# Weaving neighbouring weight blocks word by word in a two-layer kernel on one core

## What is computed

```python
# first block: modulated layers
u = h @ w_in                       # layer 0: gated linear recurrence
mix = (recurrence(conv(u)) * gelu(u)) @ w_out
x = x + g_m * mix
x = x + g_f * ((silu(h @ w_gate) * (h @ w_up)) @ w_down)
q, k, v = h @ w_q, hk @ w_k, hk @ w_v   # layer 1: attention, then w_o and a second swiglu
# second block: 16 extra tokens in front (272 in all), two hybrid layers
proj = h @ w_in                    # convolution, state space, retention, stick-breaking
up = [branch_n @ w_branch[n] for n in range(4)]
mix = sum(sigmoid(gate_n) * up_n) @ w_out
f = (silu(h @ w_ffn_gate) * (h @ w_ffn_up)) @ w_ffn_out
```

## Time and profile before

| | |
|---|---|
| median of three executions | 2205.68 us (2205.02 to 2208.81) |
| span of the profiled execution, first to last instruction | 2205.2 us |
| TensorE busy with matmuls | 2182.8 us, 99% of the span |
| TensorE busy with weight loads | 2129.4 us, 97% |
| DVE / ACT busy | 1542.7 us (70%) / 1169.5 us (53%) |
| moved by DMA | 428.19 MB, mean 194 GB/s |

### The profile page before, as it was taken

The page is one execution under the profiler, slowest core; times in us unless marked ns, Lnnn a source line. Parts: engine busy times, 40 slices in busy tenths (PEclk is TensorE's granted clock), DMA queues, the critical chain, the costliest instruction groups (busy, mean ns, idle before and its releaser), DMA issues.

```text
span 2205.2 us, 40768 instructions
## 1 busy us (share of the span) xinstructions
PE 2182.8 (99%) x17030; PEld 2129.4 (97%) x17030; DVE 1542.7 (70%) x2584; ACT 1169.5 (53%) x1950; POOL 2.2 (0%) x6
## 2 busy tenths in 40 slices
PE   8999999999999999999999999999999999999999
PEld 6899999999999999999999999999999999999998
DVE  6878997776577678755655865596879556657663
ACT  3645544564544567446644644454866456546443
POOL 0000000000000000000000000000000000000000
PEclk9999999999999999999999999999999999999999
DMA  8869996376655555444355555555654544455653
GB/s 344 313 220 397 386 357 245 115 239 223 180 182 171 192 170 158 151 146 144 118 167 170 166 174 163 162 194 189 194 169 148 174 128 130 153 182 173 188 175 115
DMA packets 123190, 428.19 MB, mean 194 GB/s; under 512 B 14528, under 2 KB 18816, under 8 KB 122368
## 3 DMA queue, kind: packets, MB, share of 16 engines
q1 hardware_dynamic: 123008, 425.58, 58.5%
HBM read 422.87 MB, written 2.66 MB: 193 GB/s over the span
## 4 chain that ended last, share of the span: by engine, by line
PE 91%; DVE 4%; ACT 2%; DMA 1%; issue 1%; SPq 0%; ACTq 0%; DVEq 0%
PE stream L513 26%; PE stream L515 25%; PE stream L514 25%; PE stream L529 5%; PE side L709 2%; PE side L716 1%; DVE w_lo L424 1%; PE side L529 1%; DMA mod_raw_first<-in_mod_w 1%; PE side L638 1%; PE side L850 0%; DMA raw<-in_ffn_up 0%; PE stream L520 0%; PE stream L521 0%; PE stream L525 0%
## 5 line engine op out<-in xcount | busy, mean ns | idle before, releaser
L513 PE MATMUL stream<-h_hi,w_hi 128*128 128x272 f32 (+1 forms) x3280 | 946.2, 288 | 0.7 <-DVE h_lo L1735 0.5
L515 PE MATMUL stream<-h_hi,w_lo 128*128 128x272 f32 (+1 forms) x3280 | 937.0, 286 | 0.0
L514 PE MATMUL stream<-h_lo,w_hi 128*128 128x272 f32 (+1 forms) x3280 | 934.5, 285 | 0.0
L424 DVE TENSOR_TENSOR w_lo<-raw,w_hi 128x1024 fp32r<-128x1024 f32 (+1 forms) x642 | 769.4, 1206 | 145.6 <-ACT w_hi L979 144.1
L979 ACT CAST w_hi<-raw 128x1024 fp32r<-128x1024 f32 (+1 forms) x642 | 654.3, 1035 | 245.9 <-DMA raw<-in_ffn_down 90.2
L513 PEld LDWEIGHTS stream<-h_hi,w_hi 128*128 128x128 f32 x3280 | 618.9, 189 | 3.9 <-DVE h_lo L1735 1.6
L515 PEld LDWEIGHTS stream<-h_hi,w_lo 128*128 128x128 f32 x3280 | 619.0, 189 | 0.0
L514 PEld LDWEIGHTS stream<-h_lo,w_hi 128*128 128x128 f32 x3280 | 618.0, 188 | 0.5
L513 PE MATMUL stream<-f_hi,w_hi 128*128 128x256 f32 (+1 forms) x704 | 199.1, 283 | 0.0
L515 PE MATMUL stream<-f_hi,w_lo 128*128 128x256 f32 (+1 forms) x704 | 198.7, 282 | 0.0
L514 PE MATMUL stream<-f_lo,w_hi 128*128 128x256 f32 (+1 forms) x704 | 198.2, 282 | 0.0
(11 more groups left out here) (390 smaller groups left out, 3058.2 us busy)
## 6 DMA issues: line engine op xcount, KB each, us to landing
raw<-in_ffn_up SPq DMA_DIRECT2D x176, 512.0 KB, 3.8
mod_raw<-in_mod_w SPq DMA_DIRECT2D x96, 512.0 KB, 5.4
raw<-in_ffn_down SPq DMA_DIRECT2D x64, 512.0 KB, 3.8
raw<-in_a_cx SPq DMA_DIRECT2D x32, 512.0 KB, 3.9
raw<-in_up_a SPq DMA_DIRECT2D x32, 512.0 KB, 3.5
raw<-in_up_b SPq DMA_DIRECT2D x32, 512.0 KB, 3.5
raw<-in_b_kq SPq DMA_DIRECT2D x32, 512.0 KB, 3.5
raw<-in_up_c SPq DMA_DIRECT2D x32, 512.0 KB, 3.5
```

The source lines that it names most:

```text
L424: eng.tensor_tensor(w_lo[:, x.slot, 0:x.kb * P], raw[:, x.slot, 0:x.kb * P], w_hi[:, x.slot, 0:x.kb * P].bitcast(F32), ALU.subtract).then_ ...
L513: pe.matmul(ps, w_hi[:, x.slot, W], rhs[0][:, k, off:off + n], start=first, stop=False)
L514: pe.matmul(ps, w_hi[:, x.slot, W], rhs[1][:, k, off:off + n], start=False, stop=False)
L515: return pe.matmul(ps, w_lo[:, x.slot, W], rhs[0][:, k, off:off + n], start=False, stop=last)
```

## The change

A new host function `woven` takes the place of `chunks` for all phases that split their weights: q, attn_out, ffn_up0 to ffn_up3, ffn_down0 to ffn_down3, and everything in the second block. Blocks 2j and 2j + 1 of a chunk share a stretch of 256 words, one word of each in turn. On the chip a new helper `block` builds the access pattern of block k: 128 words with a step of 2 words, starting at word k % 2 of its pair. The three functions that issue split products use it. The DMAs, the cast and the subtraction go over whole panels as before, and the plain phases keep `chunks`.

```diff
         @block.tensor
         def _(pe):
+            def block(W, x, k):
+
+                pair = W[:, x.slot, k // 2 * 2 * P:(k // 2 + 1) * 2 * P].rearrange("p (c s) -> p c s", s=2)
+                return pair[:, :, k % 2]
+
             def three(ps, x, wcol, rhs, k, off, n, first, last):
 
-                W = slice(wcol * P, (wcol + 1) * P)
-                pe.matmul(ps, w_hi[:, x.slot, W], rhs[0][:, k, off:off + n], start=first, stop=False)
-                pe.matmul(ps, w_hi[:, x.slot, W], rhs[1][:, k, off:off + n], start=False, stop=False)
-                return pe.matmul(ps, w_lo[:, x.slot, W], rhs[0][:, k, off:off + n], start=False, stop=last)
+                high, low = block(w_hi, x, wcol), block(w_lo, x, wcol)
+                pe.matmul(ps, high, rhs[0][:, k, off:off + n], start=first, stop=False)
+                pe.matmul(ps, high, rhs[1][:, k, off:off + n], start=False, stop=False)
+                return pe.matmul(ps, low, rhs[0][:, k, off:off + n], start=False, stop=last)
...
+def woven(w, kb=8):
+
+    k, m = w.shape
+    w = w.reshape(k // (kb * P), kb // 2, 2, P, m // P, P)
+    return w.transpose(4, 0, 3, 1, 5, 2).reshape(-1, P, kb * P)
+
+
...
-    a["q"], a["attn_out"] = chunks(f["attn_w_q"][0]), chunks(f["attn_w_o"][0])
+    a["q"], a["attn_out"] = woven(f["attn_w_q"][0]), woven(f["attn_w_o"][0])
     for l in range(2):
-        a[f"ffn_up{l}"] = pairs(chunks(f["ffn_w_gate"][l]), chunks(f["ffn_w_up"][l]))
-        a[f"ffn_down{l}"] = chunks(f["ffn_w_down"][l], FT)
+        a[f"ffn_up{l}"] = pairs(woven(f["ffn_w_gate"][l]), woven(f["ffn_w_up"][l]))
+        a[f"ffn_down{l}"] = woven(f["ffn_w_down"][l], FT)
```

More of the change, by code:

```diff
@@ L509, in _ @@
         def _(pe):
+            def block(W, x, k):
+                pair = W[:, x.slot, k // 2 * 2 * P:(k // 2 + 1) * 2 * P].rearrange("p (c s) -> p c s", s=2)
+                return pair[:, :, k % 2]
             def three(ps, x, wcol, rhs, k, off, n, first, last):
-                W = slice(wcol * P, (wcol + 1) * P)
-                pe.matmul(ps, w_hi[:, x.slot, W], rhs[0][:, k, off:off + n], start=first, stop=False)
-                pe.matmul(ps, w_hi[:, x.slot, W], rhs[1][:, k, off:off + n], start=False, stop=False)
-                return pe.matmul(ps, w_lo[:, x.slot, W], rhs[0][:, k, off:off + n], start=False, stop=last)
+                high, low = block(w_hi, x, wcol), block(w_lo, x, wcol)
+                pe.matmul(ps, high, rhs[0][:, k, off:off + n], start=first, stop=False)
+                pe.matmul(ps, high, rhs[1][:, k, off:off + n], start=False, stop=False)
+                return pe.matmul(ps, low, rhs[0][:, k, off:off + n], start=False, stop=last)
             def high_two(ps, x, wcol, rhs, k, off, n, first):
-                W = slice(wcol * P, (wcol + 1) * P)
-                pe.matmul(ps, w_hi[:, x.slot, W], rhs[0][:, k, off:off + n], start=first, stop=False)
-                pe.matmul(ps, w_lo[:, x.slot, W], rhs[0][:, k, off:off + n], start=False, stop=False)
+                pe.matmul(ps, block(w_hi, x, wcol), rhs[0][:, k, off:off + n], start=first, stop=False)
+                pe.matmul(ps, block(w_lo, x, wcol), rhs[0][:, k, off:off + n], start=False, stop=False)
             def low_one(ps, x, wcol, rhs, k, off, n, last):
-                return pe.matmul(ps, w_hi[:, x.slot, wcol * P:(wcol + 1) * P], rhs[1][:, k, off:off + n], start=False, stop=last)
+                return pe.matmul(ps, block(w_hi, x, wcol), rhs[1][:, k, off:off + n], start=False, stop=last)
             def plain(ps, x, wcol, rhs, k, off, n, first, last):
@@ L2266, in layout @@
         rq, rk, rv, rg, bq, bk, bv, gates = (take(n) for n in (D,) * 7 + (4 * D,))
-        a[f"a_cx{l}"], a[f"a_b{l}"] = pairs(chunks(c), chunks(x)), chunks(b)
-        a[f"dt{l}"] = chunks(np.concatenate([dt, np.zeros((D, P - 16), dt.dtype)], axis=1))
+        a[f"a_cx{l}"], a[f"a_b{l}"] = pairs(woven(c), woven(x)), woven(b)
+        a[f"dt{l}"] = woven(np.concatenate([dt, np.zeros((D, P - 16), dt.dtype)], axis=1))
         for n, v in (("s_x", xs), ("s_bc", bc), ("s_z", z), ("r_v", rv), ("r_q", rq), ("r_k", rk), ("r_g", rg),
                      ("b_v", bv)):
-            a[n + str(l)] = chunks(v)
-        a[f"b_kq{l}"] = pairs(chunks(bk), chunks(bq))
+            a[n + str(l)] = woven(v)
+        a[f"b_kq{l}"] = pairs(woven(bk), woven(bq))
         for j, n in enumerate("abcd"):
-            a[f"up_{n}{l}"] = pairs(chunks(gates[:, j * D:(j + 1) * D]), chunks(f["w_branch_2"][l, j]))
-        a[f"mix_out{l}"] = chunks(f["w_out_2"][l])
+            a[f"up_{n}{l}"] = pairs(woven(gates[:, j * D:(j + 1) * D]), woven(f["w_branch_2"][l, j]))
+        a[f"mix_out{l}"] = woven(f["w_out_2"][l])
         up = f["w_ffn_in_2"][l]
-        a[f"ffn_up{2 + l}"] = pairs(chunks(up[:, :FF]), chunks(up[:, FF:]))
-        a[f"ffn_down{2 + l}"] = chunks(f["w_ffn_out_2"][l], FT)
+        a[f"ffn_up{2 + l}"] = pairs(woven(up[:, :FF]), woven(up[:, FF:]))
+        a[f"ffn_down{2 + l}"] = woven(f["w_ffn_out_2"][l], FT)
     return {n: np.ascontiguousarray(v) for n, v in a.items()}
```

## The result

The changed kernel takes 2216.97 us (median of four, 2215.47 to 2218.07) against 2205.8 us of the kernel before on the same chip. The ratio is 1.0048, with a 95% interval from 1.0036 to 1.0059: about 11 us slower. That lies inside the forecast range and on the wrong side of no change.

What follows compares the result with a forecast made beforehand. It took the pace of split matmuls on TensorE as the bound. Removing half the 9.5 ns excess, 4.75 ns x 15,216 loads = 72 us, gave 2205.2 - 72 = 2133 us; range 2060 to 2325.

Steps and rivals of the forecast that it cites:

- Pace as the bound, and the excess: Split matmuls on TensorE set the end; each step costs 9.5 ns on average over a clean one.
- Where that excess comes from: In split steps: weight load and moving read, running together, get into each other's way, making the 9.5 ns excess.
- a fixed price: First rival: changing weights in a split step costs a fixed amount, so nothing changes, 2205 us; chance 0.20.
- the term of 72 us: Woven loads of split products remove half the excess: 4.75 ns x 15,216 = 72 us.
- The clean step: Split step without excess: its columns at 2.4 GHz plus 2.4 ns, so 109.1 ns at 256 columns, 115.7 at 272.
- the best end: Lower bound for the split loads: all the excess goes, 15,216 x 9.5 ns = 145 us, to 2060 us.
- The slower load: Rival on woven weight loads: the strided load itself takes longer and sets the step, 3666 us; chance 0.12.
- The third rival: Strided load gets a word every second cycle, occupying the loader 218 ns instead of 109; 3666 us, chance 0.12.
- two signs for the loader as the bound: Either loads get longer than 189 ns, or the stages with 256 and 272 columns come to the same pace.
- More collisions: Second rival: woven loads meet the moving read more often, mean step over 118 and 125.8 ns; 2215 to 2350 us, chance 0.20.
- Cast, subtraction, transfers, waits: Panel work on ACT and DVE (1035 and 1206 ns each), DMAs and waits stay as before: nothing.
- A wider spread of steps: Stage means may spread: walking abreast, a split step should depend more on its pair of buffers than before.

Runs made afterwards that it cites:

- half_plain: Kernel before, contiguous weights, with the second and third product of each block cut to the first 128 token columns; 2113.99 us.
- reps: Kernel before, each block's second product replaced by six with 64 weight columns, three of 128 and three of 192 moving columns; 3896.9 us.
- short64: Kernel before, contiguous weights, with the second product of each block loading only 64 of its 128 weight columns; 2198.55 us.
- short32: Kernel before, contiguous weights, with the second product of each block loading only 32 of its 128 weight columns; 2195.94 us.
- same_word: Kernel before, contiguous weights, with the second and third product of each block reading one token column over and over; 2133.01 us.
- half_woven: Changed kernel, woven weights, with the second and third product of each block cut to the first 128 token columns; 2182.22 us.
- cut240: Kernel before, contiguous weights, second and third product of each block 16 token columns fewer; 2142.09 us, and 2193.38 us for the same cut with woven weights.
- only272: Kernel before with weights woven only in the stages of 272 token columns; 2203.78 us against 2205.93, ratio 0.9989.

## Why the prediction was wrong

**Pace as the bound, and the excess: right.** The end is still set by the pace of split matmuls, and the means over all pairs, 118.12 and 125.85 ns, repeat the prediction's 118.0 and 125.8. The excess of some 9.5 ns is real. Only "the next pair starts when both are through" doesn't hold for single records, as half_plain shows; it does for the mean pace.

**"Where that excess comes from": the step that failed.** The prediction put it down to the load and the moving read getting into each other's way, because traffic and a slow load were excluded, a fixed price was left as a rival, and one pair of stages differed by 1.4 ns. The list was not complete. A price for each moving column was missing from it, since the two lengths at hand, 256 and 272, were so near each other that 8.9 and 10.1 looked like one number. Yet its own 7.8 ns for 16 more columns, 0.49 ns each where 2.4 GHz gives 0.42, pointed there. reps excludes a fixed price, short64 and short32 show that shorter loads take 2 to 3 ns off a block where collisions would have taken 4.75 and 7.1, and same_word that the excess is there only when new moving words are read. What part the load may have in it, walking abreast didn't give back: at 272 columns, where the longer load stays hidden, a step fell by 0.36 ns where the forecast needed 4.75. Weaving changes neither the number of moving words nor their place, so the term of 72 us had almost nothing to remove. (The clean step, too, was taken 2.4 ns over its columns where lru_y's count gave 2.2; nothing hangs on that.) lru_y, the row that pointed to the best end, may be clean for another reason than walking abreast: its columns come at half the rate. That is argued, not shown; no run changed it.

**The slower load: right in kind, mis-sized.** The third rival took an occupancy of 218 ns from a word every second cycle; half_woven shows 117 to 118, so 8 to 9 ns more and not 109. The prediction did say that it decides at 118. The woven load lands just there. In 256-column steps two chains of equal length, 118.1 ns of columns and 117 to 118 ns of loading, now have to meet in each step, and the mean is 119.7, above both; that the later of two uneven times sets the step is how I read it, and no run shows it directly. cut240 bears on it from the side: with 16 columns fewer in two of three products, weaving costs 4.4 ns a step instead of 1.6. In 272-column steps 125.85 covers the load, and there is no loss. So of the prediction's two signs for the loader as the bound the longer loads came, and the stages did not come to one pace, because 272 columns still take longer than the load.

On this, the Trainium skill, page "SBUF — State Buffer", section "Specifications (TRN2)", asks for two hits in each 16-byte line for full bandwidth, and says that each cross to a new line pays a penalty. The runs agree in kind, with the jump between a step of two words (197 ns) and of four (330). But a woven load, with two hits in each line and twice as many lines, takes 196 to 197 ns against 189; the prediction went by the two hits alone and kept 109 ns. The measurement decides, and the 8 to 9 ns more of occupancy made the loss. The same page's "Who interferes with whom" gives TensorE two independent read ports; short32 agrees only in the main, as a load of a quarter took 2.9 to 3.0 ns off the three steps of a block.

**More collisions: not the cause.** The condition of that rival, a mean step over 118, was met in the 256-column stages, but half_woven shows the same 7 to 9 ns with half as much moving read beside the load, and the 272-column stages became faster.

**Cast, subtraction, transfers, waits: right.** TensorE's longest waits are 6.9 and 1.8 us, and its loader waits for w_lo for 0.4 us in all (0.5 before). Both steps over a panel take as long as in the earlier trace rows, by the page's groups of the kernel after:

```profile
L424 DVE TENSOR_TENSOR w_lo<-raw,w_hi 128x1024 fp32r<-128x1024 f32 (+1 forms) x642 | 769.8, 1206 | 146.4 <-ACT w_hi L983 145.1
L983 ACT CAST w_hi<-raw 128x1024 fp32r<-128x1024 f32 (+1 forms) x642 | 654.8, 1035 | 251.5 <-DMA raw<-in_ffn_down 89.9
```

**A wider spread of steps: wrong.** The prediction expected a step to depend more on its pair of buffers. At 272 columns the standard deviation of the steps fell from 2.70 to 2.05 ns, at 256 it stayed (2.32 and 2.29), and ffn_up2 and ffn_down2, 1.4 ns apart before, are 0.2 apart now.

**Left open.** Why 272-column steps gain 0.36 ns; whether the 2 to 3 ns that short loads save in a block, and the 1.4 ns between those two stages, are one collision that weaving eases a little; and why a moving column costs 0.4625 ns and not 0.4167.

## What to carry to other kernels

Before a change is bet on an overhead, find out what the overhead scales with, over lengths far enough apart to tell a fixed price from one for each column; here two kernels, one with short products and one with short loads, would have shown it. An engine that is hidden still has a budget: the loader had 118 - 109 = 9 ns of cover, and a layout that lengthens each load by 8 used it up, so the same layout costs nothing where steps are longer (only272) and almost five times as much, 51 us, where they are 16 columns shorter in two of three products (cut240). In this kernel weaving paid only where the moving side outlasts the woven load (125.85 ns against 117 to 118), and then 0.1% of the time; at a step of four words loads start 233 ns apart, far over every step here.

## What the hardware showed unexpectedly

- A load of 128 weight columns takes 189 ns contiguous, 197 with a step of two words, 330 with four and 339 with eight: a small price, then a jump, then almost nothing more. Start to start, where nothing else binds, it takes 109 to 111, 117 to 118, 233 and 240 ns.
- float32r matmuls with a weight load beside each follow one another at about 0.4625 ns a column from 128 to 272 columns (59.5, 89.8, 118.1 and 125.9 ns) at a granted clock of 1.00, 11% over 1 / 2.4 GHz. At 272 columns they fall to 115.6 to 116.3 ns, 2 to 3 over 272 / 2.4 GHz, when the moving operand is one column read again and again.
